# Eleven more transposed blocks by way of VectorE's squares and transfers within SBUF, and two loads in squares

## What is computed

```python
def hybrid_layer(x, ...):                     # first block
    p = rms_norm(x, norm_w) @ w_in            # q, k, v of four branches, z, gates
    for b in range(4):                        # dsa, fox, diff, dil
        y = branches[b].reshape(...) * silu(z_parts[b])
        merged += sigmoid(g_parts[b]) * (y @ w_branch[b])
    return x + merged @ w_out                 # then rms_norm(final_norm_w)

def second_block(x, p, ...):
    y = _rms(h, norm_mix_g)
    z = y @ w_in_2                            # input of the four mixers
    oa = _mixer_sgu(...)                      # einsum with tril(sgu_w): 4 heads of 128x128
    h = h + concatenate([oa, ob, oc, od]) @ w_out_2
    y = _rms(h, norm_ffn_g)
    h = h + (silu(y @ w_gate) * (y @ w_up)) @ w_down
    y = _rms(h, norm_ple_g)
    h = h + sigmoid(y @ w_ple_gate) * (p @ w_ple_proj)   # p: the side input, 256x256
    return _rms(h, final_norm_g)
```

## Time and profile before

| | |
|---|---|
| median of 3 runs | 2067.35 us (2067.28 to 2067.61) |
| the profiled execution's own time | 2066.91 us |
| its span, first to last instruction | 2064.8 us |
| mean granted TensorE clock | 0.998 |
| TensorE busy | 2045.4 us, 99% |
| VectorE busy | 1567.9 us, 76% |
| ScalarE busy | 1040.9 us, 50% |
| GpSimd busy | 99.3 us, 5% |
| moved by DMA | 403.61 MB, mean 195 GB/s |

### The profile page before, as it was taken

How to read it: one execution, slowest core, us unless ns; L and a number is a source line. 1 busy time by engine, 2 the same in 40 slices (tenths; PEclk the granted TensorE clock), 3 DMA queues, 4 the chain that set the end, 5 groups by cost and what they waited for, 6 DMA issues and landing times.

```text
span 2064.8 us, 24955 instructions
## 1 busy us (share of the span) xinstructions
PE 2045.4 (99%) x10311; PEld 1739.1 (84%) x10311; DVE 1567.9 (76%) x1461; ACT 1040.9 (50%) x982; POOL 99.3 (5%) x200
## 2 busy tenths in 40 slices
PE   9999999999999999999999999999999999999998
PEld 8888888888888888888999987888888888888887
DVE  6576555765688888855789859989888889888565
ACT  6444443544455555545344445645455545555453
POOL 2000000000000000000000000111110011110000
PEclk9999999999999999999999999999999999999999
DMA  8655555555565655655655566666566666666461
GB/s 252 215 183 175 166 169 184 164 183 178 189 211 204 222 203 184 219 204 183 210 184 165 182 204 209 230 213 194 192 220 227 211 207 194 201 225 224 145 234 59
DMA packets 229857, 403.61 MB, mean 195 GB/s; under 512 B 13763, under 2 KB 59067, under 8 KB 229489
## 3 DMA queue, kind: packets, MB, share of 16 engines
q1 hardware_dynamic: 221344, 387.64, 56.7%
q0 software_dynamic: 7648, 13.26, 2.2%
q10 hardware_dynamic: 752, 1.12, 0.2%
HBM read 394.62 MB, written 2.12 MB: 192 GB/s over the span
## 4 chain that ended last, share of the span: by engine, by line
PE 89%; DVE 8%; ACT 1%; issue 1%; DMA 1%; ACTq 0%; SPq 0%; DVEq 0%
PE psA L714 20%; PE psA L716 20%; PE psA L715 20%; PE psA L921 6%; PE psB L714 5%; PE psB L715 5%; PE psB L716 5%; PE psA L925 3%; DVE lo L1721 3%; DVE CA L2031 1%; DVE raw L1738 1%; PE psB L979 1%; ACT hi L1252 1%; DVE lo in Y L1721 1%; DMA X<-in_x_dram 0%
## 5 line engine op out<-in xcount | busy, mean ns | idle before, releaser
L1721 DVE TENSOR_TENSOR lo<-raw,hi 128x2048 fp32r<-128x2048 f32 (+2 forms) x364 | 822.7, 2268 | 262.5 <-ACT hi L1252 260.7
L1252 ACT ACTIVATE hi<-raw 128x2048 fp32r<-128x2048 f32 (+2 forms) x364 | 689.2, 1899 | 456.3 <-PE psA L716 300.2
L714 PE MATMUL psA<-hi,XHL 128*128 128x512 f32 x1008 | 393.8, 391 | 1.7 <-DVE XHL L1822 1.7
L716 PE MATMUL psA<-hi,XHL 128*128 128x512 f32 x1008 | 390.9, 388 | 0.0
L715 PE MATMUL psA<-lo,XHL 128*128 128x512 f32 (+1 forms) x872 | 337.7, 387 | 0.0
L714 PE MATMUL psA<-hi,YHL 128*128 128x512 f32 x624 | 244.3, 392 | 0.0
L716 PE MATMUL psA<-hi,YHL 128*128 128x512 f32 x624 | 243.0, 389 | 0.0
L714 PEld LDWEIGHTS psA<-hi,XHL 128*128 128x128 f32 x1008 | 189.4, 188 | 40.9 <-issue 2.1
L716 PEld LDWEIGHTS psA<-hi,XHL 128*128 128x128 f32 x1008 | 189.3, 188 | 39.2
L715 PE MATMUL psA<-lo,YHL 128*128 128x512 f32 x536 | 208.6, 389 | 0.0
L715 PEld LDWEIGHTS psA<-lo,XHL 128*128 128x128 f32 x872 | 163.9, 188 | 32.2
(11 more groups left out here) (435 smaller groups left out, 2891.6 us busy)
## 6 DMA issues: line engine op xcount, KB each, us to landing
raw<-in_w_in_dram SPq DMA_DIRECT2D x149, 1024.0 KB, 5.1
raw<-in_w_up_dram SPq DMA_DIRECT2D x35, 1024.0 KB, 5.2
raw<-in_w_gate_dram SPq DMA_DIRECT2D x35, 1024.0 KB, 5.2
raw<-in_w_out_dram SPq DMA_DIRECT2D x32, 1024.0 KB, 5.1
raw<-in_w_down_dram SPq DMA_DIRECT2D x32, 1024.0 KB, 5.1
raw<-in_w_ple_gate_dram SPq DMA_DIRECT2D x14, 1024.0 KB, 5.1
raw<-in_w_branch_dram SPq DMA_DIRECT2D x13, 1024.0 KB, 5.1
raw in Y<-in_w_down_dram SPq DMA_DIRECT2D x12, 1024.0 KB, 5.1
```

The lines of the kernel that those rows point to most:

```text
L714: e.matmul(dst, A2[0], B2[0], start=first, stop=False, skip_group_check=True)
L716: return e.matmul(dst, A2[1], B2[0], start=False, stop=last, skip_group_check=True)
L1252: e.activation(hi[u % H][:, 0:m], raw[slot][:, 0:m], ACT.Copy).then_inc(hi_made, 1)
L1721: e.tensor_tensor(lo[slot][:, 0:m], raw[slot][:, 0:m], hi[u % H][:, 0:m].bitcast(F32), ALU.subtract).then_inc(lo_made, 1)
```

## The change

Eleven more turns become moved turns: the attention outputs 0, 1 and 2 (the squares stand at the old unit, the high and low parts four units later, `MOVEDA`), and the quarters f = 0, 1, 2 of FIRST and of SECOND and f = 0, 1 of THIRD (`MOVEDX`). The squares of X are made in `post`, right behind the quarter's sum; they and the moved block lie in a tile `squares in X` that shares the space of `XHL`: in the part of f=3 for f = 0 and 2, in that of f=2 for f=1 (`spare`). The high and low parts of f stand at `OUT+8+4f` and `OUT2+8+4f`, where the turn stood at +6+4f; those of THIRD at five units behind the quarter's last. The turn of f=3 stays TensorE's, at +18 as before; in the last stage the two turns that stay (f = 2, 3) are four and three units behind their quarter. Because the norm's scale differs for each block of 128 channels, the low part is eight instructions of 128x128. `squares_moved` becomes two semaphores that the moves use in turn. The input forms of the feed-forward move from `OUT2+10` to `OUT2+12`. The spatial weights arrive in four transfers and the side input in eight, laid out by squares, and VectorE's one square transpose each replaces TensorE's four transposes. Waits of `attend` for an earlier turn become waits for the earlier branch's heads.

The diff, cut to its core:

```diff
+        with ExitStack() as here:
+            in_X = sb("squares in X", [128, 4, 2, 1024], F32, here)
...
+        PT2 = blocks[3][0][:, 512:1024].rearrange("p (k t) -> p k t", k=2)
...
         def landed_square(n):
-            return 256 * (MOVES.index(n) + 1)
+            i = MOVES.index(n)
+            return squares_moved[i % 2], 256 * (i // 2 + 1)
+
+        def by_squares(x):
+
+            return x.rearrange("p (r k t c) -> p r k t c", r=4, k=4, t=2)
         def turning(b):
-            return blocks[b][0][:, 1024:2048].rearrange("p (r k t c) -> p r k t c", r=4, k=4, t=2)
+            return by_squares(blocks[b][0][:, 1024:2048])
+
+        def spare(f):
+
+            return in_X[:, (3, 2, 3)[f], :, :]
         def moved(x):
-            return flat(x).rearrange("p (q m c) -> p m q c", q=4, m=8)
+            return x.rearrange("p (q m c) -> p m q c", q=4, m=8)
...
-        MOVES = tuple(HIDDEN + j for j in range(10))
+        MOVES = (0, 1, 2, FIRST, FIRST + 1, FIRST + 2, SECOND, SECOND + 1, SECOND + 2) + tuple(HIDDEN + j for j in range(10)) + (THIRD, THIRD + 1)
...
+        MOVEDA = {42: 0, 53: 1, 76: 2}
...
-        TURN1 = {OUT + 6 + 4 * f: f for f in range(4)}
-        TURN2 = {OUT2 + 6 + 4 * f: f for f in range(4)}
+        TURN1 = {OUT + 18: 3}
+        TURN2 = {OUT2 + 18: 3}
...
-        TURN3 = {named["down", LAST_DOWN + f].last + 2: f for f in range(4)}
+        TURN3 = {named["down", LAST_DOWN + f].last + 6 - f: f for f in (2, 3)}
+        MOVEDX = {OUT + 8 + 4 * f: (FIRST, f, 16) for f in range(3)}
+        MOVEDX.update({OUT2 + 8 + 4 * f: (SECOND, f, 32) for f in range(3)})
+        MOVEDX.update({named["down", LAST_DOWN + f].last + 5: (THIRD, f, 48) for f in range(2)})
...
-        SUMS = OUT2 + 10
+        SUMS = OUT2 + 12
...
-            def move(n, b, dst):
-
-                squares, to = turning(b), flat(dst[:, :, :]).rearrange("p (q n) -> p q n", q=4)
+            def move(n, squares, dst):
...
-                                    squares[32 * q:32 * q + 32, r, :, :, :]).then_inc(squares_moved, 16)
+                                    squares[32 * q:32 * q + 32, r, :, :, :]).then_inc(landed_square(n)[0], 16)
+
+            def move_x(first, f):
+                move(first + f, by_squares(spare(f)[:, 0, :]), spare(f)[:, 1, :])
...
-            e.dma_start(B[:, 1, 0:512].rearrange("p (h s) -> p h s", h=4),
-                        A["sgu_w_2"][0].rearrange("h t s -> t h s")).then_inc(mixers_landed, 16)
-
+            for r in range(4):
+                e.dma_start(B[32 * r:32 * r + 32, 1, 0:512].rearrange("p (m c) -> p m c", m=16),
+                            A["sgu_w_2"][0][:, :, 32 * r:32 * r + 32].rearrange("h (q i) s -> i (h q) s", i=32)
+                            ).then_inc(mixers_landed, 16)
...
-            e.dma_start(PP[:, :, :], A["p_2"][0, 0].rearrange("(t p) c -> p t c", p=128)).then_inc(p_landed, 16)
+            for r in range(4):
+                for k in range(2):
+                    c = 128 * k + 32 * r
+                    e.dma_start(PP[32 * r:32 * r + 32, k, :].rearrange("p (m c) -> p m c", m=8),
+                                A["p_2"][0, 0][:, c:c + 32].rearrange("(m i) c -> i m c", i=32)).then_inc(p_landed, 16)
...
-                        e.wait_ge(flip_low, b)
+                        e.wait_ge(logits_read, job)
...
-                if u in ATTENDED:
-                    attended(ATTENDED[u])
+                if u in ATTENDED and ATTENDED[u] == 3:
+                    attended(3)
...
-                if u == MIXERS + 5:
-                    e.wait_ge(mixers_landed, 5 * 16)
-                    e.wait_ge(sb_made, 1)
-                    for h in range(4):
-                        x = e.transpose(psB[:, 0, 128 * h:128 * h + 128], B[:, 1, 128 * h:128 * h + 128], ID[:, :])
-                    x.then_inc(sw_turned, 1)
...
-                if u == P_TURN:
-                    ps = psB[:, 1, 0:512].rearrange("p (k t) -> p k t", k=2)
-                    e.wait_ge(p_landed, 16)
-                    e.wait_ge(flip_low, HIDDEN + 11)
-                    for k in range(2):
-                        for t in range(2):
-                            x = e.transpose(ps[:, k, 128 * t:128 * t + 128], PP[:, t, 128 * k:128 * k + 128], ID[:, :])
-                    x.then_inc(p_turned, 1)
...
-                e.wait_ge(squares_moved, landed_square(n))
-                e.activation(ordered(dst), moved(src[:, :, :]), ACT.Copy, scale=scale).then_inc(flip_high, 1)
+                e.wait_ge(*landed_square(n))
+                if isinstance(scale, list):
+                    for k in range(4):
+                        x = e.activation(dst[:, k, :].rearrange("p (t q c) -> p t q c", t=2, q=4),
+                                         src.rearrange("p (q k t c) -> p k t q c", q=4, k=4, t=2)[:, k, :, :, :],
+                                         ACT.Copy, scale=scale[k])
+                    x.then_inc(flip_high, 1)
+                    return
...
+                if u in MOVEDX:
+                    first, f, g = MOVEDX[u]
+                    high_moved(first + f, XH[:, 4 * f:4 * f + 4, :], spare(f)[:, 1, :], scale_cols(g, f))
...
+            def turn_x_squares(f):
+
+                for t in range(2):
+                    turn_squares(cols(f), by_squares(spare(f)[:, 0, :]), t)
...
+                if isinstance(scale, list):
+                    to, h = [x.rearrange("p k (t q c) -> p k t q c", t=2, q=4) for x in (dst, dstH.bitcast(F32))]
+                    m = src.rearrange("p (q k t c) -> p k t q c", q=4, k=4, t=2)
+                    for k in range(4):
+                        for t in range(2):
+                            x = e.scalar_tensor_tensor(out=to[:, k, t, :, :], in0=m[:, k, t, :, :], scalar=scale[k],
+                                                       in1=h[:, k, t, :, :], op0=ALU.mult, op1=ALU.subtract)
+                    x.then_inc(flip_low, 1)
...
+                if u in ATTENDED and ATTENDED[u] < 3:
                     b = ATTENDED[u]
                     if b == 2:
+                        e.wait_ge(diff_scaled, 1)
+                    else:
+                        e.wait_ge(heads_read, heads_before(b, 4))
+                    for t in range(2):
+                        turn_squares(YN, turning(b), t)
...
+                if u in MOVEDX:
+                    first, f, g = MOVEDX[u]
+                    kb = slice(4 * f, 4 * f + 4)
+                    low_moved(first + f, XL[:, kb, :], XH[:, kb, :], spare(f)[:, 1, :], scale_cols(g, f))
...
-                    e.wait_ge(sw_turned, 1)
-                    e.tensor_tensor(SW[:, :, :], psB[:, 0, 0:512].rearrange("p (h s) -> p h s", h=4),
+                    e.wait_ge(mixers_landed, 8 * 16)
+                    finish(e.transpose(B[:, 1, 512:1024], B[:, 1, 0:512]))
+                    e.tensor_tensor(SW[:, :, :], B[:, 1, 512:1024].rearrange("p (h s) -> p h s", h=4),
...
+                if u == P_TURN - 1:
+                    e.wait_ge(p_landed, 8 * 16)
+                    e.wait_ge(unit_done, done(("S", 10)))
+                    e.transpose(flat(PT2), flat(PP[:, :, :])).then_inc(p_turned, 1)
                 if u == P_TURN:
                     e.wait_ge(ph_made, 1)
-                    e.tensor_tensor(PL, psB[:, 1, 0:512].rearrange("p (k t) -> p k t", k=2), PH.bitcast(F32),
-                                    ALU.subtract).then_inc(pt_made, 1)
+                    e.tensor_tensor(PL, PT2, PH.bitcast(F32), ALU.subtract).then_inc(pt_made, 1)
...
+                    if n < 3:
+                        e.wait_ge(h_made, n + 1)
+                        turn_x_squares(n)
...
+                    if n < 3:
+                        e.wait_ge(bank_dve, g.freed)
+                        turn_x_squares(n)
...
+                    if n in (LAST_DOWN, LAST_DOWN + 1):
+                        e.wait_ge(bank_dve, g.freed)
+                        turn_x_squares(f)
```

More of the change, by code:

```diff
@@ L443, in build_hybrid @@
         form_made, sf_sum, sf_high, sf_low = [sem(n) for n in ("form_made", "sf_sum", "sf_high", "sf_low")]
-        squares_turned, squares_moved = sem("squares_turned"), sem("squares_moved")
+        squares_turned, squares_moved = sem("squares_turned"), [sem(f"squares_moved{i}") for i in range(2)]
         sum_copied, gate_made, up_made, gates_ready = [sem(n) for n in ("sum_copied", "gate_made", "up_made", "gates_ready")]
@@ L685, in gpsimd_program @@
             e.dma_start(BT[:, :, :], bass.AP(scratch.tensor, scratch.offset, [[1, 128], [384, 12], [1, 256]])).then_inc(bt_landed, 16)
+            for b in range(3):
+                move(b, turning(b), flat(YN[:, :, :]))
             e.wait_ge(flip_turned, turned(MERGED + 3))
@@ L691, in gpsimd_program @@
                     e.dma_start(FW[:, :], rows(A["final_norm_w"], 2048)).then_inc(fw_landed, 16)
+            for f in range(3):
+                move_x(FIRST, f)
             e.wait_ge(unit_done, done(("out", 3)))
@@ L1400, in side @@
```

(24 more changed lines are left out.)

45 lines of the change are left out of this document (26 added, 19 removed).

## The result

The changed kernel takes 2071.32 us in the median of 17 runs (2069.10 to 2072.31), the kernel before 2067.28 (2066.48 to 2067.72, 17 runs): a ratio of 1.0019 (95% interval 1.0012 to 1.0025), 4.0 us slower. The forecast was 2069.4 with no change, 2060.5 to 2074. The sign is clear of noise, and the size stands just inside the 0.2% that I called no change.

What follows compares the result with a forecast made beforehand. TensorE's stream plus its gaps was taken as the bound. Turns and loads removed (-5.3, -0.4, -1.8) and A +2.7, B +5.4, C +1.5 gave +2.1 on 2067.35: 2069.4 us, range 2060.5 to 2074.

Steps and rivals of the forecast that it cites:

- Gain: Work taken off TensorE: eleven turns, 9.7 us, and the two small groups, 0.9 us; 10.6 us in all.
- two small groups: Four transposes of the spatial weights and four of the side input leave TensorE, 0.43 us each.
- B: Start of the first up/gate block: waits of 2.3 us for `x` and 6.1 at f=3's turn; net +5.4 us (+3.6 to +7.2).
- A: Start of the mixers: TensorE's turn of f=3 waits for the low part of FIRST f=2, +2.7 us (2.2 to 3.3).
- C: Last stage: waits of 4.1 us at f=2's turn and 0.9 at f=3's; net +1.5 us (0.5 to 3).
- the main case: Gain and new waits nearly cancel: 2069.4 us, forecast as no change (2063.2 to 2071.5), chance 0.53.
- the first rival: TensorE's clock falls to 1.2 GHz behind the new holes at B and C: 2071.5 to 2073.5 us, chance 0.15.
- Rivals 2 and 3: 2: B keeps its old time, 2064.0 us, chance 0.19; 3: no new wait at all, 2055.6 us, chance 0.09.
- Rival 4: Transfers of moved blocks come late and block ScalarE's queue: 2075 us or more, chance 0.04.

Runs made afterwards that it cites:

- fill_all: Like fill, plus 8 products for nothing before the turn at the mixers and 7 ahead of `x`: 2069.33 us, ratio 1.0010.
- again: The changed kernel run once more with no edit: 2071.41 us, ratio 1.0018 to the kernel before.
- fill: The changed kernel with products for nothing before two late turns, 23 in the first up/gate block and 13 in the last stage: 2070.23 us, ratio 1.0013.
- third_on_pe: The changed kernel with the two moved THIRD turns back on TensorE at their old places: 2068.78 us, ratio 1.0008.
- f2_on_pe: The changed kernel with the turns of f=2 of FIRST and SECOND back on TensorE at unit +14: 2065.13 us, ratio 0.9990.
- early: The changed kernel with high and low parts of f=2 of FIRST and SECOND at unit +14 in place of +16: 2070.64 us, ratio 1.0015.

## Why the prediction came out as it did

**Gain.** Right. 0.88 a turn was forecast and 0.90 measured (mean of nine in the ledger), 0.43 for each of the two small groups and 0.36 measured: 10.6 us forecast, 10.7 by these figures.

**The three places.** The waits were forecast as 2.7, 2.3, 6.1 and 4.1 us and came as 2.53, 2.23, 5.92 and 4.02. Each comes from the instruction that was named: VectorE's row scales, its backlog behind the input forms, ScalarE's squares ahead of the high part. VectorE at B: I put the low part of f=2 at 33.4 behind the start of unit 12, and it starts at 1261.59, 33.4 behind 1228.2. Only the 0.9 us wait at the turn of f=3 in the last stage didn't come in the first profile; the slow products had used the time, and in fill_all, without them, it is there (0.7).

**The sum.** It says +2.1 us. In its own terms the first profile reads: six turns ahead of A -5.5, A +2.6, spatial weights -0.3, two SECOND turns -1.8, B +6.0, C +2.3, and -0.6 for an old wait that the sum left alone: +2.7. The profile of fill_all, where the clock doesn't fall, has B +5.2 and C +1.4 against the forecast's +5.4 and +1.5, and ends at +1.5. So the chain was sized well, a little high in each term. That 2069.4 is the time of the lower group is partly chance. 1.2 us of half clock were not in the sum. Against them stand terms 0.6 too high and 0.3 us outside the spans (2.1 us before, 1.8 after); and I had added to 2067.35, the median of all runs, while the profiled run of the lower group has the fast start.

**Where it was low.** The step is the choice of the main case over the first rival: that "no row shows what 6 us do", with a chance of 0.15 for a fall of the clock. It fell, at C's 4.0 us as at B's 5.9. The rival put it at 2071.5 to 2073.5, and the median is 2071.3. Its sizes were too high at B and C (1.2 us together by fill_all, not 2.7 to 4.1), since the slow stretch lay partly within the hole and was shorter than the half unit, twelve products, that it took: some six products at B and three at C. At B it also took the place of the 1.7 us wait at `p3`. It missed the third place: behind A's 2.5 us the clock falls in three of the four profiles with that hole (again, fill, third_on_pe) and costs 1.6 us; the times suggest most executions. The slow start, 0.8 us with what follows it, probably belongs to both kernels. "It decides once a hole is long enough, and needs B's hole to be near 6 us" was wrong: 2.2 to 2.9 us were enough in some executions (fill, f2_on_pe, again), and 3.6 us in early were not. The advice of the Trainium skill (TensorE: Matmul & The Clock Gate, Why this matters for your kernels) against idle gaps had deserved more weight than a trace that could show none. Here the traces agree with it at the two long holes, with 0.65 and 0.78 granted around them, and don't agree with it for every hole: 1.00 behind 2.5 us in the first profile and behind 3.6 us in early.

**Rivals 2 and 3.** Both fell: B cost 6.0 us in the terms of the sum, 0.9 of it half clock, and none of the three orders was harmless.

**Rival 4.** ScalarE waits for no transfer of a moved block in the changed kernel, but the slack is smaller than I thought. Medians, from issue to landing:

```profile
HB<-raw in Y POOLq DMA_DIRECT2D x160, 32.0 KB, 1.7
squares in X<-squares in X POOLq DMA_DIRECT2D x128, 32.0 KB, 4.0
```

The prediction took the median of the single transfers, 1.7 us, for the landing of the last one, and a move for 10 us. From the first issue to the last landing a move took 10.9 to 13.1 us already in the kernel before, and a move of X takes 9.0 to 13.6 in the changed one. This is what early ran into: the move of FIRST f=2 took 11.9 us there, from 952.8 to 964.7, and ScalarE's wait ends at 964.8. The issue takes what it took (498 ns each), so the figure of 3.1 us a transfer that the Trainium skill gives beside two-port copies of VectorE (SBUF — State Buffer, SBUF: two separate sides) isn't seen here either.

**Where the gain went.** In the first profile TensorE's busy time fell by 7.7 us: 10.7 went, and 3.0 came back, most of it products and turns at half clock. Its idle time between the first and the last product rose by 10.4: 14.7 of new waits, less 4.3 of old ones (1.7 at `p3`, 1.0 at the THIRD turn, the rest in four waits of 0.4 to 0.9, gone or shorter). Together that is the 2.7 us between the spans. The cost of half clock in full is larger than the 1.2 us by which fill_all is ahead, since part of the slow time only takes the place of old waits. Built up from the other side, each part with its reading in time: attention turns and loads 3.6 us (2067.1 to 2063.5), three moved turns of FIRST and SECOND 2.4 (to 2061.1), two THIRD turns read one unit earlier 3.0 (to 2058.1).

## What to carry to other kernels

Work taken off the busiest engine pays only where what replaces it is read no later: for each block that now comes by another way, count in the order of each engine what stands ahead of its last step, and give back those whose slack is gone. Six of the eleven moved turns gained 6 us where all eleven cost 4, and with the last stage's two read one unit earlier it is 9. Count a hole in TensorE's stream with the slow products that may follow it: here the shortest that had them was 2.2 us, and they cost 1.6 us behind one of 2.5. For a block that comes by transfers, take the landing of the last transfer, not the median of all.

## What was not expected of the hardware

- A hole of 2 to 4 us in TensorE's stream is followed by products at half clock in some executions and not in others: 1.00 granted at 980 to 985 in one profile of the changed kernel, 0.88 and then 0.78 in the next, with the same wait of 2.5 us; 0.73 behind one of 2.2 us in fill, 1.00 behind one of 3.6 us in early.
- Products for nothing during a wait keep the clock at 1.00, and took 2.1 us off the median (2071.41 to 2069.33) though the operands came no earlier.
- At the start TensorE reaches full speed at 9.8 to 10.1 us in seven of the thirteen profiles and at 10.6 to 11.7 in the other six, which then stand 0.4 to 0.9 us behind the profile of the kernel before at 20 us.
- The sixteen transfers of a move, 32 KB each within SBUF, land in a median of 1.7 to 5.6 us at the same issue rate. It isn't the tile alone: the first move of HB has 4.2 in the kernel before, too. It goes with the DMA share of the stretch: 1.7 to 2.1 us where the share is 0.45 to 0.49, 2.9 to 4.4 at 0.63 to 0.77, 4.1 at 0.95 and 5.6 at 1.05, all in the first profile of the changed kernel. No run changed that traffic.
